# Two expert layers: the last items' low parts, row additions and output tiles in another order

## The reference, cut to what matters

```
def hier_moe(xn, w_grp, b_grp, w_exp, b_exp, w1, w3, w2):
    t = xn.reshape(-1, dm)
    ...            # a softmax over 4 groups picks one group; of its 4 experts the best two are taken
    gate = jnp.sum(jax.nn.one_hot(eid, N_EXPERTS, dtype=jnp.float32) * w_tok[..., None], axis=1)
    hid = jax.nn.silu(jnp.einsum('td,edf->tef', t, w1)) * jnp.einsum('td,edf->tef', t, w3)
    hid = hid * gate[..., None].astype(hid.dtype)
    y = hid.reshape(t.shape[0], N_EXPERTS * EXP_FF) @ w2.reshape(N_EXPERTS * EXP_FF, dm)
    return y.reshape(bsz, s, dm).astype(xn.dtype)
```

## Time and profile before

| | us |
|---|---|
| median of 3 runs | 1217.92 (1217.58 to 1219.41) |
| the profiled execution, its own time | 1217.04 |
| its span, first to last instruction | 1215.3 |
| mean granted TensorE clock, share of full speed | 0.988 |
| busy in the span: PE | 1173.7 (97%) |
| DVE | 719.7 (59%) |
| ACT | 590.3 (49%) |
| POOL | 361.1 (30%) |
| chain that ended last, by engine | PE 85%, DVE 7%, ACT 2%, DMA 2% |

### The profile page before, as it was taken

How to read it: one execution, slowest core, us unless ns; L and a number is a source line. 1 busy time by engine, 2 the same in 40 slices (tenths; PEclk the granted TensorE clock), 3 DMA queues, 4 the chain that set the end, 5 groups by cost and what they waited for, 6 DMA issues and landing times.

```text
span 1215.3 us, 15456 instructions
## 1 busy us (share of the span) xinstructions
PE 1173.7 (97%) x5272; PEld 869.2 (72%) x5272; DVE 719.7 (59%) x1281; ACT 590.3 (49%) x1134; POOL 361.1 (30%) x320
## 2 busy tenths in 40 slices
PE   8999999999999899999899999989999998999996
PEld 5467876788777566666678887768887775666665
DVE  4797533322422688888745992772223236888887
ACT  2733246455634266655535364453456342666661
POOL 2034440564222011113136664263342220111130
PEclk9999999999999999999999999999999999999999
DMA  9432231277102799997232230012322018999963
GB/s 294 141 139 78 32 114 70 93 293 306 70 1 95 308 404 380 389 379 283 76 130 78 70 117 23 2 70 74 134 70 70 1 70 322 394 374 393 377 237 126
DMA packets 77643, 214.92 MB, mean 177 GB/s; under 512 B 23620, under 2 KB 24560, under 8 KB 65272
## 3 DMA queue, kind: packets, MB, share of 16 engines
q1 hardware_dynamic: 64688, 180.22, 40.0%
q0 software_dynamic: 10048, 28.92, 6.5%
q10 hardware_dynamic: 2840, 4.91, 1.1%
HBM read 187.90 MB, written 32.51 MB: 181 GB/s over the span
## 4 chain that ended last, share of the span: by engine, by line
PE 85%; DVE 7%; ACT 2%; DMA 2%; issue 2%; SPq 1%; DVEq 0%; ACTq 0%
PE bank L853 40%; PE bank L1212 7%; PE bank L1245 7%; PE bank L1217 6%; PE bank L1073 2%; PE bank L1095 2%; PE bank L891 2%; PE bank L826 2%; PE bank L1154 1%; PE bank L1201 1%; PE bank L1122 1%; PE bank L1034 1%; PE bank L1268 1%; SPq L611 1%; DVE h L2491 1%
## 5 line engine op out<-in xcount | busy, mean ns | idle before, releaser
L684 POOL TENSOR_TENSOR wlo<-W,whi 128x512 fp32r<-128x512 f32 x176 | 256.3, 1468 | 444.4 <-ACT whi L1477 426.3
L1477 ACT ACTIVATE whi<-W 128x512 fp32r<-128x512 f32 x176 | 108.1, 631 | 243.8 <-PE bank L853 225.6
L853 PE MATMUL bank<-whi,xTr 128*128 128x512 f32 x480 | 193.4, 403 | 0.9 <-ACT E L1941 0.7
L853 PE MATMUL bank<-wlo,xTr 128*128 128x512 f32 x416 | 162.9, 391 | 0.0
L853 PEld LDWEIGHTS bank<-whi,xTr 128*128 128x128 f32 x480 | 90.8, 189 | 21.8 <-POOL wlo L684 1.7
L853 PE MATMUL bank<-whi,E4r 128*128 128x512 f32 x256 | 99.8, 390 | 0.0
L1217 PE MATMUL bank<-E4r,E1r 128*128 128x512 f32 x360 | 98.5, 422 | 0.0
L1245 PE MATMUL bank<-whi,E2r 128*128 128x512 f32 x256 | 89.3, 410 | 7.4 <-DVE E2r L2452 5.9
L853 PEld LDWEIGHTS bank<-wlo,xTr 128*128 128x128 f32 x416 | 78.7, 189 | 16.6 <-issue 1.2
L2043 DVE TENSOR_TENSOR h<-bank,h 128x512 f32<-128x512 f32 x32 | 21.8, 692 | 115.0 <-PE bank L853 115.0
L1217 PEld LDWEIGHTS bank<-E4r,E1r 128*128 128x128 f32 x360 | 67.6, 188 | 27.0 <-issue 7.4
(11 more groups left out here) (498 smaller groups left out, 2422.7 us busy)
## 6 DMA issues: line engine op xcount, KB each, us to landing
E<-in_moe_w SPq DMA_DIRECT2D x48, 1024.0 KB, 11.5
W<-in_moe_w SPq DMA_DIRECT2D x32, 1024.0 KB, 9.7
xT<-in_moe_w SPq DMA_DIRECT2D x16, 1024.0 KB, 14.3
W<-in_od_w_in SPq DMA_DIRECT2D x7, 2048.0 KB, 8.4
ybuf<-E SPq DMA_DIRECT2D x26, 512.0 KB, 8.1
ybuf<-memV POOLq DMA_DIRECT2D x12, 1024.0 KB, 19.9
W<-in_w_mem_kv SPq DMA_DIRECT2D x4, 2048.0 KB, 9.3
W<-in_xa_wq SPq DMA_DIRECT2D x4, 2048.0 KB, 7.8
```

What stands on the lines that cost most here:

```text
L684: pool.tensor_tensor(wlo[s_ % RING][:, :], slot(name)[:, block_of(name, k), :], whi[s_ % RING][:, :].bitcast(F32), ALU.subtract).then_inc( ...
L853: ins = pe.matmul(bank(u + t)[:, :], a, b, start=(k == 0 and n == 0), stop=(k == KT - 1 and n == 2))
L1477: act.activation(whi[s_ % RING][:, :], slot(name)[:, block_of(name, k), :], ACT.Copy).then_inc(S["w_hi"], 1)
```

## The change

The row additions, the one-hots and the ends of the token tiles are moved in DVE's list; `to_tokens` and `down` in PE's; the silu of item 3 and its parts in ACT's. The last item's `down` takes its weight parts from the buffers `up_hi` and `up_lo`, which the last `up` has read by then, in the place of the ring. Matmuls, parts, row additions and one-hots are as many as before, and of the same shapes. The part of the diff that only cuts functions in pieces is left out.

```diff
+        end_whi, end_wlo = up_hi[0:4], up_lo[0:4]
...
-                            wh, wl = whi[2 * half + k], wlo[2 * half + k]
+                            wh, wl = (end_whi, end_wlo) if late == LATE - 1 else (whi, wlo)
+                            wh, wl = wh[2 * half + k], wl[2 * half + k]
...
                     turn_hidden(q, 2, last=True)
-                    down(q, 2, late=1)
                     pe.wait_ge(S["late_onehots"], l + 1)
                     pe.wait_ge(m["xt_ready"], q * (2 * SLOTS) + 2 * SLOTS)
                     to_tokens(0, 0)
                     pe.wait_ge(m["hid_ready"], q * SLOTS + 3)
                     to_tokens(0, 1)
+                    down(q, 2, late=1)
                     turn_hidden(q, 3, last=True)
+                    down(q, 3, late=2)
                     to_tokens(1, 0)
                     to_tokens(1, 1)
-                    down(q, 3, late=2)
-                    for n in range(2):
-                        to_tokens(n, 2)
-                    for t in range(3):
-                        to_tokens(2, t)
+                    to_tokens(0, 2)
+                    to_tokens(1, 2)
+                    to_tokens(2, 0)
+                    to_tokens(2, 1)
+                    to_tokens(2, 2)
                     for n in range(3):
                         to_tokens(n, 3)
...
                 item(last_quad, 0)
-                for n in range(LATE):
-                    item(last_quad, SLOTS - LATE + n, late=n)
+                item(last_quad, 1, late=True)
+                gated_hidden(last_quad, 2)
+                down_high(last_quad, 2, [w[:, :] for w in whi])
+                gated_hidden(last_quad, 3)
+                hidden_high(last_quad, 2)
+                down_high(last_quad, 3, end_whi)
+                late_high(last_quad, 2, 1)
+                hidden_high(last_quad, 3)
+                late_high(last_quad, 3, 2)
...
-                def late_onehots():
+                def late_tokens():
 
                     dve.wait_ge(S["late_cols"], 2 * l + 2)
-                    s3 = v3(slot_of_row, LATE)
-                    v(tt(s3, last(late_tok, TT), mid(tile_row, LATE), ALU.subtract))
-                    for n in range(LATE):
-                        ins = tt(late1h[:, n, :].rearrange("p (t a) -> p t a", t=TT), mid(iof[:, :], TT),
-                                 last(s3[:, n, :], P), ALU.is_equal)
-                    ins.then_inc(S["late_onehots"], 1)
+                    v(tt(v3(slot_of_row, LATE), last(late_tok, TT), mid(tile_row, LATE), ALU.subtract))
+
+                def late_onehot(n):
+
+                    return tt(late1h[:, n, :].rearrange("p (t a) -> p t a", t=TT), mid(iof[:, :], TT),
+                              last(v3(slot_of_row, LATE)[:, n, :], P), ALU.is_equal)
...
+                def add_late(t):
+
+                    dve.wait_ge(S["late_filled"], TT * l + t + 1)
+                    for half, b in enumerate(token_banks[t]):
+                        hs = h[:, t, half * 512:(half + 1) * 512]
+                        ins = tt(hs, banks[b][:, :], hs, ALU.add)
+                    ins.then_inc(m["h_combined"], 1)
+
                 def last_turn(q):
 
                     hidden(q, 0)
                     low_parts(q, 0)
                     output(q, 0)
+                    late_tokens()
+                    late_onehot(0)
+                    late_onehot(1).then_inc(S["late_onehots"], 1)
                     hidden(q, 1)
                     low_parts(q, 1)
-                    late_onehots()
                     late_low(0, 0)
                     late_low(0, 1)
+                    hidden(q, 2)
+                    down_low(q, 2, *ring, last=True)
+                    late_onehot(2)
                     add_row(0, 0)
+                    hidden_low(q, 2, last=True)
+                    hidden(q, 3)
+                    down_low(q, 3, end_whi, end_wlo, last=True)
+                    late_low(1, 0)
+                    late_low(1, 1)
+                    hidden_low(q, 3, last=True)
                     add_row(0, 1)
-                    hidden(q, 2)
-                    low_parts(q, 2, last=True)
                     add_row(1, 0)
-                    late_low(1, 0)
                     add_row(1, 1)
-                    late_low(1, 1)
-                    hidden(q, 3)
-                    low_parts(q, 3, last=True)
+                    dve.wait_ge(m["y_stored1"], q * (8 * SLOTS))
+                    late_low(2, 0)
+                    late_low(2, 1)
+                    add_late(0)
                     add_row(2, 0)
+                    add_late(1)
                     add_row(2, 1)
                     add_row(3, 0)
-                    dve.wait_ge(m["y_stored1"], q * (8 * SLOTS))
-                    late_low(2, 0)
+                    add_late(2)
                     add_row(3, 1)
-                    late_low(2, 1)
-                    for t in range(TT):
-                        dve.wait_ge(S["late_filled"], TT * l + t + 1)
-                        for half, b in enumerate(token_banks[t]):
-                            hs = h[:, t, half * 512:(half + 1) * 512]
-                            ins = tt(hs, banks[b][:, :], hs, ALU.add)
-                        ins.then_inc(m["h_combined"], 1)
+                    add_late(3)
```

More of the change, by code:

```diff
@@ L1777, in rows_high, with gated_hidden, down_high @@
                     act.activation(xg_hi, xgT[:, KT - SPLIT:KT, :], ACT.Copy).then_inc(m["hi_parts"], 1)
-                def item(q, j, late=None):
-                    par = j % 2
-                    last = late is not None and j > 1
+                def gated_hidden(q, j):
                     act.wait_ge(m["hid_filled"], q * SLOTS + (j + 1))
-                    act.activation(silu[par], banks[2 + par][:, 0:FF], ACT.Silu).then_inc(m["silu_ready"], 1)
+                    act.activation(silu[j % 2], banks[2 + j % 2][:, 0:FF], ACT.Silu).then_inc(m["silu_ready"], 1)
+                def down_high(q, j, dst):
                     act.wait_ge(m[f"w2_{j}"], q * 16 + 16)
@@ L1794, in item @@
[L1794 to L1804 removed]
+                    act.activation(hThi[j % 2], banks[4][:, 0:2 * P], ACT.Copy).then_inc(m["hi_parts"], 1)
@@ L1805, in item @@
+                def item(q, j, late=False):
+                    par = j % 2
+                    gated_hidden(q, j)
+                    down_high(q, j, [w[:, :] for w in whi])
+                    up_high(q, j + 2, 0, 2)
+                    hidden_high(q, j)
+                    up_high(q, j + 2, 2, SPLIT)
+                    rows_high(q, j + 2)
+                    if late:
+                        late_high(q, j, 0)
                         return
```

44 lines of the change are left out of this document (21 added, 23 removed).

## The result

| | us |
|---|---|
| before, median of 5 runs | 1217.92 (1217.21 to 1223.47) |
| after, median of 5 runs | 1211.84 (1211.32 to 1215.80) |
| ratio after to before, 95% interval | 0.9947 (0.9926 to 0.9968) |
| the profiled execution of after: its own time, span, mean granted clock | 1215.80, 1214.0, 0.985 |

The change made the kernel 0.5% faster. A second comparison of twelve runs gave 1211.51 and 0.9956 (0.9940 to 0.9972).

A forecast was written before the change was run, and what follows sets the result against it. PE bounds the kernel, each layer's end being a chain through DVE. Gains of 1.45 (layer 1) and 2.6 (layer 0), 4.1 in sum, less 2.7 for the clock leave 1.4: 1217.92 to 1216.5, range 1213.8 to 1219.0.

The forecast's parts named there:

- The schedule: Last quad of each layer, ordered through DVE: layer 1 gains 1.45 us, layer 0 2.6.
- One-hots at nothing: DVE ahead of item 1's hidden product: moving the token subtraction and two one-hots (1.40) away gains nothing, being covered by waits.
- the gap ahead of `down` 3: PE at each layer's end: a new idle time of 2.0 us while it waits for item 3's `hTlo`.
- the six microseconds: Layer 1: PE's last item starts at 1193.0 against 1198.5; mostly lost, as half the row additions move behind it.
- 608.86: Microseconds by which layer 0's list was taken to run earlier than layer 1's, from the first matmul of `down` 2.
- With every matmul at the full clock: Both layers' gains summed before any charge for PE's clock: 4.1 us.
- The charge for the gap of 2.0: PE's new gap in each layer: at two in four, one slow clock stretch counted for both, costing 1.7 us.
- The charge for the long gap: Layer 0, 3.8 us PE gap ahead of 18 transposes: these run at half speed, costing 0 to 1.6, taken as 1.0.
- (c): Rival: layer 0's long gap keeps the clock low into the first projection; slower, 1220.6 or 1219.0; chance 0.13.
- (d): Rival: DVE's order delays POOL's gathers or puts ACT's silu 3 before `hThi`; each at most 0.5; no separate chance.
- The median 0.88 above the profile: Whole kernel: runs' median 0.88 above the profiled 1217.04; the gain of 1.4 was subtracted from that median, 1217.92.

The follow-up runs named there:

- after_filled: After with thrown-away matmuls ahead of `down` 3 (1.4 us, both layers) and ahead of layer 0's transposes (2.7 us): 1210.02, ratio to before 0.9962.
- before_both: Before with layer 0's item 0 store ahead of the panel load, and 1.8 us of thrown-away matmuls ahead of `down` 2 in both layers: 1212.15, ratio 0.9949.
- repeat_after: After, unchanged, timed and profiled again: 1211.51 over 12 runs, ratio to before 0.9956.
- rows_in_gap: After with row additions (2,0) and (2,1) ahead of the first token tile, in DVE's idle time: 1207.52, ratio to before 0.9931.
- rows_panel: After with row additions (2,0) and (2,1) ahead of the first tile, and layer 0's item 0 store ahead of the panel load: 1206.35, ratio to before 0.9907.
- rows_first: After with all four remaining row additions ahead of the first token tile: 1209.92, ratio to before 0.9936.
- after_panel: After with layer 0's item 0 store issued ahead of the panel load: 1211.30, ratio to before 0.9941.
- layer0_only: Before with the new order in layer 0 alone, the old one in layer 1: 1214.11, ratio to before 0.9966.
- layer1_only: Before with the new order in layer 1 alone, the old one in layer 0: 1215.62, ratio to before 0.9984.
- repeat_before: Before, unchanged, timed against itself and profiled again: 1217.69 over 12 runs, ratio 1.0002.
- before_panel: Before with layer 0's item 0 store issued ahead of the 2 MB panel load on SP's queue: 1214.25, ratio 0.9970.
- last_in_ring: After with the last item's weight parts put back in the ring of four: 1219.43, ratio to before 1.0036.
- before_filled: Before with 1.8 us of thrown-away matmuls between `turn_hidden` 2 and `down` 2 in both layers: 1213.06, ratio 0.9978.

## Why the prediction was wrong, point by point

**The schedule: right.** One-hots at nothing: the stretch ahead of `turn_hidden` 1 is not longer. DVE's idle time ahead of the first tile 2.4 forecast, 2.36 measured; the gap ahead of `down` 3 2.0, 1.68; none between tiles; `down` 3 at 1193.02, 1193.25; the end 1210.8, 1211.0. From `turn_hidden` 1 to the end of layer 1 the gain was 1.72, forecast 1.45; in layer 0 at full clock 39.79 - 37.10 = 2.69 (after_filled), forecast 2.6. In layer 0 the gap ahead of the transposes was 3.40, forecast 3.8: by the forecast's own prices PE's last 24 token matmuls end at 596.0 and not at 595.7, so the sum should have given 3.5. Two more figures are slips without effect: the six microseconds by which `down` 3 comes earlier are 5.5, and 608.86 is 608.83.

**"With every matmul at the full clock" 4.1: mislabelled.** I set a new order at full clock against the profile of before with its two slow stretches. These cost 16.47 - 14.83 = 1.64 in layer 0 and 9.42 - 8.50 = 0.92 in layer 1. At full clock on both sides, and with gathers that cost nothing, the old order has 38.14 in layer 0 (before_both) and 10.89 + 8.50 + 16.31 = 35.70 in layer 1; the new one 37.10 (after_filled) and 34.96. So the order alone is worth 1.04 + 0.74 = 1.8, and 4.1 less 2.56 is 1.5. The same slip made the expectation of before_both too large.

**The charge for the gap of 2.0, 1.7: wrong.** This is the first step that failed, "at two in four I count one slow stretch for both: 1.7". Of the gaps of 1.68 in the new order none was followed by a slow stretch, in 14 layer ends of eight profiles (after, repeat_after, rows_in_gap, rows_panel, rows_first and after_panel twice each, layer0_only and layer1_only once). Of the gaps of 2.21 ahead of `down` 2 in the old order, seven of eight were (before, repeat_before, before_panel, layer0_only, layer1_only); the one without was the 580.28 of the earlier trace rows, half of my sample of gaps without one. The old order's second gap (1.73 to 1.78) was followed by one in 2 of 12 layer ends, both of them ends whose first gap had had none (t3-turn 16.47 in before, t3-end 17.96 in before_both, against 14.83 and 16.31). So the two gaps of an end hardly look like two draws of the same kind, as I had taken them: the first is nearly always slow, the second was slow in two of the four ends without a slow stretch behind the first and in none of the other eight. Twelve ends are few for that. I pooled them and carried their mean to a gap in another place, which then measured 1.68, shorter than both. Without this charge the forecast would have been 1214.8.

**The charge for the long gap, 1.0: right.** A slow stretch in eight of eight unfilled profiles (after, repeat_after, layer0_only, rows_in_gap, rows_panel, rows_first, after_panel, last_in_ring). turn-proj is 5.11 to 5.58 with it and 4.50 without: 0.6 to 1.1. The projection was not touched, so (c) fell: in 605.20 to 608.60 PE did nothing but transposes, and the clock was full behind them. The Trainium skill, "TensorE: Matmul & The Clock Gate", section "Part 4: PE-mode transpose", says that transposes don't count as busy as matmuls do, by which (c) would have been the likeliest case; this trace doesn't agree.

**(d), POOL's gathers late, "bounded by 0.5": wrong.** This is the second step that failed. The change itself put timely gathers 0.7 later (5.5 against 4.75), at no cost. But the step looked only at what the new order does to the gathers, and found them early enough, as they are. It didn't ask whether the old order loses by them in executions that I had not seen. The mean of t1-t2 in the old order's three profiles is 13.2 against 10.91: 2.3 us, of which the new order pays 0.4 in the mean (t2-t3 4.79, 4.78 and 5.97).

**The median 0.88 above the profile, gain put on it: the form in which both failures came in.** Against the profile of before the new order gains 39.79 - 38.43 = 1.36 and 36.66 - 34.96 = 1.70, together 3.1, where I had 1.4; the difference is the 1.7 charged for gaps that brought nothing. The rest up to 5.4, 2.3 us, is by how much the old order's ends are worse in the mean (41.97 and 36.81) than in that profile (39.79 and 36.66). That profile had drawn a good end of layer 0 and lost as much elsewhere: repeat_before has 4.35 more in its two ends and a span that is 0.3 shorter. So the account of the 5.4 is: the old order loses 41.97 - 38.14 + 36.81 - 35.70 = 4.9 in the mean to late gathers and the clock, the new one 38.43 - 37.10 = 1.3, and the order alone gives 1.8. With before_panel and before_filled each giving 0.2 to 0.3% on the old order, and both 0.5%, the runs bear this out: most of the change's gain is these two losses removed, a clock stretch and a DMA wait, and the smaller part a shorter list.

What stays open: why SP's queue is behind in some executions, with the same loads 4 to 5 us later; why the clock falls behind gaps of 2.2 us and not behind 1.68; and how the time is split between the two losses in the mean, since a late gather brings a slow stretch with it.

## What to carry to other kernels

One profile gives the schedule to some tenths of a microsecond but says nothing of how often a wait or a slow stretch occurs: before an edit is priced, profile the kernel before two or three times, and price the old order's losses by their mean. Ask of each reordering not only what it adds, but which irregular wait (a DMA's landing, a gap behind which the clock may fall) it takes off PE's path. A store whose landing someone awaits goes ahead of a bulk load on the same queue. Where an engine's own list bounds the end, put its ready work ahead of work that isn't ready.

## What the runs showed of the hardware

- PE gaps in these layer ends, the clock behind them: behind 1.68 us it stayed full in 14 of 14 cases; behind 1.73 to 1.78 us it fell to about 0.50 in 2 of 12, behind 1.93 us in the one case, behind 2.21 us in 7 of 8, behind 2.74 to 4.87 us in 12 of 12. In two of the seven (layer 0 of repeat_before and layer1_only) it had fallen already behind the gap of 4.14 or 3.53 just ahead. Fills of 1.8 and 2.7 us took these stretches away in five of six ends; the sixth is layer 0 of before_filled, where the gathers were late.
- Transposes of 128x128 alone, on PE for 3.4 us, were followed by the full clock.
- A store of 512 KB issued 9.7 us behind a 2 MB load on the same queue landed 1.2 to 1.3 us after that load in 11 of 11 profiles, 2.7 to 8.9 us after its own issue; issued ahead of it, 3.1 us after its issue in 5 of 5.
- DVE row additions of 128x1024 with two operands in SBUF take 1.28 us alone and 2.2 to 2.3 where POOL is at work on its subtractions (also two operands in SBUF), which go from 5.0 to 8.9 us for four. An addition that starts ahead of POOL's part keeps 1.28 to 1.39, and the part beside it takes 2.3 in the place of 1.3 (rows_first, after). Of the two, the one that starts later takes longer; DVE's additions with an operand in PSUM are not slowed. The Trainium skill, "GPSIMD Engine Reference", section "1. Specifications", names this contention with DVE instructions that have two SBUF inputs; the trace agrees.
